# Attention of two transformer blocks: scores issued two steps ahead and between the transposes, loads that hold both heads, reciprocals read with a step of zero

## The reference

```python
def attend(q, k, v, mask, sink):            # first block, both branches
    s = einsum('bqkgd,bskd->bkgqs', q, k) * HEAD_DIM ** -0.5
    if mask is not None: s = where(mask, s, NEG_INF)
    if sink is not None:                    # second branch: one more logit per head
        p = softmax(concat([s, sink]))[..., :-1]
    else:
        p = softmax(s)
    return einsum('bkgqs,bskd->bqkgd', p, v)
# first branch: 8 heads of 64, each query against 512 + 256 keys
# second branch: a window of +-128 keys in blocks of 128, plus the 256 context keys
# layer 0 also attends with the 256 context queries against the 256 context keys
# second block: banded_attention over three dilations (4 heads of 64), combined by their
#   log-denominators, which is one softmax over all their keys; and 8 heads of 96 over 512 keys
```

## Time and profile before

| | |
|---|---|
| median of three executions | 3915.13 us |
| the profiled execution: its time, its span | 3911.86 us, 3910.1 us |
| PE / PEld busy | 3537.8 us (90%) / 2360.5 us (60%) |
| DVE / ACT / POOL busy | 31% / 26% / 5% |
| mean granted TensorE clock | 0.957 |
| scores L1035, PE | 800 matmuls on fp32 data, 167.7 us in the costliest group |
| transposes L1089, PE | 832 + 128 matmuls |
| product L1133, PE | 896 + 128 matmuls |
| reciprocals L1077, DVE | 96, 97.9 us |

### The profile page before, as it was taken

How to read it: one execution, slowest core, us unless ns; L and a number is a source line. 1 busy time by engine, 2 the same in 40 slices (tenths; PEclk the granted TensorE clock), 3 DMA queues, 4 the chain that set the end, 5 groups by cost and what they waited for, 6 DMA issues and landing times.

```text
span 3910.1 us, 48121 instructions
## 1 busy us (share of the span) xinstructions
PE 3537.8 (90%) x21378; PEld 2360.5 (60%) x21378; DVE 1216.6 (31%) x1667; ACT 1020.7 (26%) x1601; POOL 200.2 (5%) x124
## 2 busy tenths in 40 slices
PE   7998889999799999989889988888879888989998
PEld 5786557667663443467658875222237764867886
DVE  3235641112410111134563342111133334344333
ACT  3524531112310000036453231000021335333222
POOL 0100000111200000001000110000001010020000
PEclk9999999999799999989999988999989989999999
DMA  6440004432159999822102324999962010323331
GB/s 211 129 130 12 1 13 132 131 113 70 54 213 383 353 355 386 334 51 81 28 1 77 96 103 166 409 409 409 409 245 70 16 48 17 92 70 88 96 97 49
DMA packets 359982, 600.84 MB, mean 154 GB/s; under 512 B 48770, under 2 KB 242656, under 8 KB 359520
## 3 DMA queue, kind: packets, MB, share of 16 engines
q1 hardware_dynamic: 357024, 596.69, 43.2%
q10 hardware_dynamic: 2752, 1.08, 0.1%
HBM read 595.62 MB, written 2.10 MB: 153 GB/s over the span
## 4 chain that ended last, share of the span: by engine, by line
PE 73%; DVE 10%; DMA 7%; ACT 6%; SPq 3%; issue 1%; POOL 0%; ACTq 0%; POOLq 0%; DVEq 0%
PE ps L554 30%; PE ps L1771 6%; PE ps L2112 4%; DMA ring<-in_w_e_up 3%; PE ps L1280 3%; PE ps L603 3%; DMA ring<-in_w_e_down 3%; SPq L2414 3%; PE ps L1774 3%; PE ps L1803 3%; ACT tmp L1062 3%; DVE sm L1044 3%; PE ps L574 2%; DVE tmp L1077 2%; PE ps L1035 2%; PE ps L1468 2%
## 5 line engine op out<-in xcount | busy, mean ns | idle before, releaser
L554 PE MATMUL ps<-xh,wh 128*128 128x512 f32 x1912 | 647.3, 377 | 39.0 <-DVE xl L1972 16.9
L554 PE MATMUL ps<-xl,wh 128*128 128x512 f32 x1912 | 633.4, 369 | 0.0
L554 PE MATMUL ps<-xh,wl 128*128 128x512 f32 x1912 | 632.2, 369 | 0.0
L529 DVE TENSOR_TENSOR wl<-ring,wh 128x1024 fp32r<-128x1024 f32 (+1 forms) x247 | 309.6, 1254 | 476.6 <-ACT wh L520 476.4
L554 PEld LDWEIGHTS ps<-xh,wh 128*128 128x128 f32 x1912 | 330.8, 190 | 129.8 <-issue 51.6
L520 ACT ACTIVATE wh<-ring 128x1024 fp32r<-128x1024 f32 (+1 forms) x247 | 258.9, 1049 | 431.2 <-PE ps L554 170.1
L554 PEld LDWEIGHTS ps<-xh,wl 128*128 128x128 f32 x1912 | 332.0, 190 | 62.6
L554 PEld LDWEIGHTS ps<-xl,wh 128*128 128x128 f32 x1912 | 330.6, 190 | 62.4 <-issue 4.3
L1771 PE MATMUL ps<-ring,arena 128*32 128x512 f32 x2048 | 269.3, 598 | 1.0 <-DVE arena L1570 1.0
L1766 PE MATMUL ps<-ring,arena 128*64 128x512 f32 x1024 | 236.1, 601 | 29.6 <-DMA ring<-in_w_e_up 14.9
L1089 PE MATMUL ps<-consts,tmp 128*128 128x128 f32 x832 | 127.2, 286 | 70.7 <-DVE arena L1146 55.6
(11 more groups left out here) (246 smaller groups left out, 4492.1 us busy)
## 6 DMA issues: line engine op xcount, KB each, us to landing
ring<-in_w_e_gate SPq DMA_DIRECT2D x128, 1024.0 KB, 9.9
ring<-in_w_e_up SPq DMA_DIRECT2D x128, 1024.0 KB, 10.0
ring<-in_w_e_down SPq DMA_DIRECT2D x128, 1024.0 KB, 11.9
ring<-in_w_in SPq DMA_DIRECT2D x116, 512.0 KB, 4.0
ring<-in_w_ada SPq DMA_DIRECT2D x96, 512.0 KB, 6.1
ring<-in_w_ff SPq DMA_DIRECT2D x64, 512.0 KB, 4.1
ring<-in_w_out SPq DMA_DIRECT2D x24, 512.0 KB, 4.1
ring<-in_w_in SPq DMA_DIRECT2D x40, 256.0 KB, 3.8
```

The source lines that it names most:

```text
L529: e.tensor_tensor(m.WL[:, o:o + many], halves.aps[s][:, 0:many], m.WH[:, o:o + many].bitcast(F32), ALU.subtract).then_inc(*lo.up(X.key, q))
L554: i = e.matmul(ps[0:M, a:b], w[:, k, 0:M], h[:, k, a:b], start=k == 0 and p == 0, stop=k == 7 and p == 2)
```

## The change

It reorders the three loops. PE begins with the scores of steps 0 and 1. In turn i it then issues the transposes of step i, the scores of step i+2, and, if a group ends at i, its product. In such a turn the last load of step i comes after the scores of i+2. ACT copies load 0 of step i and does the exponentials of step i+1. DVE copies all loads from 1 on, then does the reciprocals of step i+1 and the maximum of step i+2, then the product's multiply.

`six` is replaced by `both_heads`: load n holds blocks 2n and 2n+1 of both heads, where before load 0 held four blocks of one head. The product names for each of its terms the load up to which it must wait. The second branch keeps its loads.

The reciprocals are computed once per unit, into the column where the step's maximum stood (`small(i, 0)`), and `RC` is gone. PE reads such a column 64 times (`shares`, a broadcast, step zero) as the weights of four matmuls of 64 output rows in place of two of 128. `dve_soft` waits, before it writes that column again, for the product of the group of step i-4. The copy of the turned reciprocals to SBUF is made by ACT (`act_product`), and DVE multiplies.

```diff
@@ -1015,11 +1015,10 @@
                 s = self.steps[i][0]
                 return sm[:, 16 * (i % 4) + 4 * x:16 * (i % 4) + 4 * x + s["U"]]
 
-            def sums(self, i):
-                s, g = self.steps[i]
-                first = self.ends[g - 1] + 1 if g else 0
-                o = 128 * (i - first)
-                return self.RC[:, 256 * (g % 2) + o:256 * (g % 2) + o + 64 * s["U"]]
+            def shares(self, i, b):
+
+                t = self.small(i, 0).rearrange("p (g b) -> p b g", g=2)[:, b]
+                return [t[:, g:g + 1].broadcast_to([128, 64]) for g in (0, 1)]
 
             def last_load(self, i):
                 return len(self.steps[i][0]["loads"]) - 1
@@ -1040,6 +1039,8 @@
         def dve_soft(e, A, i):
             s = A.steps[i][0]
             mx, ng = A.small(i, 0), A.small(i, 1)
+            if i > 3:
+                e.wait_ge(*a_pv.at(A.stage, A.steps[i - 4][1]))
             e.wait_ge(*a_sc.at(A.stage, i))
...
@@ -1071,52 +1072,42 @@
             if s["sink"] is not None:
                 e.tensor_tensor(A.small(i, 2), A.small(i, 2), A.small(i, 3), ALU.add).then_inc(*a_su.up(A.stage, i))
                 e.wait_ge(*a_su.at(A.stage, i))
-            if g > 1:
-                e.wait_ge(*a_pv.at(A.stage, g - 2))
-            b = s["U"] // 2
-            e.reciprocal(A.sums(i).rearrange("p (b g r) -> p g b r", b=b, g=2),
-                         A.small(i, 2).rearrange("p (g b) -> p g b", g=2).unsqueeze(3).broadcast_to([128, 2, b, 64])).then_inc(*a_rc.up(A.stage, i))
...
+            e.reciprocal(A.small(i, 0), A.small(i, 2)).then_inc(*a_rc.up(A.stage, i))
+
+        def pe_turn(e, A, i, n):
             src = A.units(i, A.P[i % 3])
...
+            ps, when = turned.take((A.stage, i, n), turned_out(A, i, n))
+            for w in when:
+                e.wait_ge(*w)
+            for c, (u, b) in enumerate(A.steps[i][0]["loads"][n][0]):
+                e.wait_ge(*a_ex.at(A.stage, i, u))
+                x = e.transpose(ps[:, 128 * c:128 * c + 128], src[:, u, 128 * b:128 * b + 128], ident)
+            x.then_inc(*a_tr.up(A.stage, i, n))
+
+        def load_sides(A, i, n):
             blocks, dst, shape = A.steps[i][0]["loads"][n]
             ps = turned.of[A.stage, i, n][:, 0:128 * len(blocks)]
...
+            return dst, (ps.rearrange("p (c q) -> p c q", q=128) if shape is None else ps.rearrange("p (g c q) -> p g c q", g=shape, q=128))
 
         def act_turn(e, A, i):
             g = A.steps[i][1]
             if g > 1:
                 e.wait_ge(*a_pv.at(A.stage, g - 2))
...
+            dst, src = load_sides(A, i, 0)
+            e.wait_ge(*a_tr.at(A.stage, i, 0))
+            e.activation(dst, src, ACT.Copy).then_inc(*a_pt.up(A.stage, i))
 
         def dve_turn(e, A, i):
             g = A.steps[i][1]
...
             if g > 1:
                 e.wait_ge(*a_pv.at(A.stage, g - 2))
...
+            for n in range(1, A.last_load(i) + 1):
+                dst, src = load_sides(A, i, n)
+                e.wait_ge(*a_tr.at(A.stage, i, n))
+                e.tensor_copy(dst, src).then_inc(*a_tl.up(A.stage, i, n))
 
         def turned_out(A, i, n):
...
+            return a_tl.at(A.stage, i, n) if n else a_pt.at(A.stage, i)
 
         def pe_product(e, A, g):
             pv = A.groups[g]["pv"]
@@ -1124,26 +1115,31 @@
             ps, when = turned.take((A.stage, "o", g), a_ov.at(A.stage, g))
             for w in when:
                 e.wait_ge(*w)
...
+            for x, (load, heads) in enumerate(pv):
+                for i in range(first, A.ends[g] + 1):
+                    for n in range(min(load, A.last_load(i)) + 1):
+                        e.wait_ge(*turned_out(A, i, n))
                 for r0, v, pt, q0, q1 in heads:
                     e.matmul(ps[r0:r0 + 64, q0:q1], v, pt, start=x == 0, stop=x == len(pv) - 1, skip_group_check=True)
             for b in (0, 1):
...
+                i = first + b if A.ends[g] > first else first
+                e.wait_ge(*a_rc.at(A.stage, i))
+                for h, share in enumerate(A.shares(i, 0 if A.ends[g] > first else b)):
+                    x = e.matmul(ps[64 * h:64 * h + 64, 256 + 128 * b:384 + 128 * b], share, ident,
+                                 start=False, stop=True, skip_group_check=True)
             x.then_inc(*a_pv.up(A.stage, g))
 
+        def act_product(e, A, g):
+            e.wait_ge(*a_pv.at(A.stage, g))
+            if g:
+                e.wait_ge(*a_ov.at(A.stage, g - 1))
+            e.activation(rb, turned.of[A.stage, "o", g][:, 256:512], ACT.Copy).then_inc(*a_rb.up(A.stage, g))
+
         def dve_product(e, A, g):
...
             dst, many = A.groups[g]["out"]
             f = lambda t: t if many is None else t.rearrange("p (b q) -> p b q", b=many)
...
+            e.wait_ge(*a_rb.at(A.stage, g))
+            e.tensor_tensor(dst, f(turned.of[A.stage, "o", g][:, 0:256]), f(rb), ALU.mult).then_inc(*a_ov.up(A.stage, g))
 
         def pe_attention(e, A):
             n = len(A.steps)
@@ -1151,43 +1147,54 @@
                 for w in freed:
                     e.wait_ge(*w)
             turned.start(((), ()))
...
+            pe_scores(e, A, 0)
+            pe_scores(e, A, 1)
+            for i in range(n):
+                last = A.last_load(i)
+                early = last if i in A.ends else last + 1
+                for x in range(early):
+                    pe_turn(e, A, i, x)
+                if i + 2 < n:
+                    pe_scores(e, A, i + 2)
+                for x in range(early, last + 1):
+                    pe_turn(e, A, i, x)
+                if i in A.ends:
+                    pe_product(e, A, A.ends.index(i))
             read = tuple(a_ex.at(A.stage, i, A.steps[i][0]["U"] - 1) for i in (n - 2, n - 1))
             out_ = (a_ov.at(A.stage, len(A.groups) - 1),) + tuple(turned_out(A, n - 1, x) for x in range(A.last_load(n - 1) + 1))
             bank.start((read, read, read, out_))
 
         def act_attention(e, A):
             n = len(A.steps)
...
+            act_soft(e, A, 0)
+            for i in range(n):
+                if i - 1 in A.ends:
+                    act_product(e, A, A.ends.index(i - 1))
+                act_turn(e, A, i)
+                if i + 1 < n:
+                    act_soft(e, A, i + 1)
+            act_product(e, A, len(A.groups) - 1)
 
         def dve_attention(e, A):
             n = len(A.steps)
...
+            dve_soft(e, A, 0)
+            dve_soft(e, A, 1)
+            dve_sums(e, A, 0)
+            for i in range(n):
+                dve_turn(e, A, i)
+                if i + 1 < n:
+                    dve_sums(e, A, i + 1)
+                if i + 2 < n:
+                    dve_soft(e, A, i + 2)
+                if i in A.ends:
+                    dve_product(e, A, A.ends.index(i))
 
         HALF = [slice(0, 64), slice(64, 128)]
 
...
+        def both_heads(PT, qs, many):
+
+            PT = PT.rearrange("p (g c) q -> p g c q", g=2)
+            return [([(g, b) for g in (0, 1) for b in (2 * n, 2 * n + 1)], PT[:, :, 2 * n:2 * n + 2, qs], 2) for n in range(many // 2)]
...
```

More of the change, by code:

```diff
@@ L1001, in build, with __init__ @@
         class Att:
-            def __init__(self, stage, groups, P, PT, RC):
-                self.stage, self.groups, self.P, self.PT, self.RC = stage, groups, P, PT, RC
+            def __init__(self, stage, groups, P, PT):
+                self.stage, self.groups, self.P, self.PT = stage, groups, P, PT
                 self.steps = [(s, g) for g, gr in enumerate(groups) for s in gr["steps"]]
@@ L1126, in pe_product @@
                 e.wait_ge(*w)
-            for i in range(first, A.ends[g] + 1):
-                for n in range(A.last_load(i) + 1):
-                    e.wait_ge(*turned_out(A, i, n))
-                e.wait_ge(*a_rc.at(A.stage, i))
-            for x, heads in enumerate(pv):
+            for x, (load, heads) in enumerate(pv):
+                for i in range(first, A.ends[g] + 1):
+                    for n in range(min(load, A.last_load(i)) + 1):
+                        e.wait_ge(*turned_out(A, i, n))
                 for r0, v, pt, q0, q1 in heads:
@@ L1153, in pe_attention @@
             turned.start(((), ()))
-            for i in range(n + 2):
-                if i < n:
-                    pe_scores(e, A, i)
-                if i > 1 and i - 2 in A.ends:
-                    pe_product(e, A, A.ends.index(i - 2))
-                if 0 < i <= n:
-                    pe_turn(e, A, i - 1)
+            pe_scores(e, A, 0)
[11 more added lines that the diff above has]
+                    pe_product(e, A, A.ends.index(i))
             read = tuple(a_ex.at(A.stage, i, A.steps[i][0]["U"] - 1) for i in (n - 2, n - 1))
@@ L2009, in dilated_attention @@
                     groups.append(dict(steps=steps, pv=pv, out=(to, 2)))
-            return Att("ad", groups, [tmp[:, i * 1536:(i + 1) * 1536] for i in range(3)], PTD, tmp[:, 4608:5120])
```

(1 more changed line is left out.)

75 lines of the change are left out of this document (14 added, 61 removed).

## The result

The changed kernel takes 3821.25 us (median of four executions, 3817.91 to 3825.94); the kernel before took 3910.49 us in the same comparison (four executions, the three of the first section and one of 3902.24). The ratio is 0.9774 [0.9749, 0.9799]: 89 us or 2.3% faster.

A forecast was written before the change was run, and what follows sets the result against it. PE was taken to pace the four attention stages, stopping for DVE. Layer 0 -42, layer 1 -19, latent -9, dilated -1 and small things -3 gave 3911.9 - 74 = 3838 us, range 3808 to 3880.

The forecast's parts named there:

- The cause of the waits: Four attention stages: PE waits through its order and DVE's queue ahead of the multiply; about 2.2 us per layer 1 group.
- The period: First-branch group of layer 1: 9.18 + 0.16 + 0.84 = 10.2 us against 11.40, gaining 1.2 us per group.
- The wait for the multiply: Second load's transposes, layer 1 group: PE waits 0.84 us every time for the multiply to free the product's bank.
- The window pair: Second branch: two window groups take 19.9 us instead of 21.44, with 3.0 us of waits and switches left.
- The latent period: Latent stage: 9.48 - 1.67 + 0.84 + 0.16 + 0.18 = 9.0 us per group.
- The dilated stage: Dilated attention: PE is packed, so nothing gained per group and about 1 us at the ends.
- The clock: Attention stages: denser work keeps PE's granted clock at 0.98 or more; layer 0's shortfall is 15 us of full-rate time.
- A: Rival, 48 groups outside dilated: DVE becomes the bound, a load's copy late behind a reduction; 34 us lost, 3872; chance 0.14.
- B: Rival, 48 groups: clock never falls and the wait for the multiply halves; 20 us more gain, 3818; chance 0.10.
- C: Rival, reciprocal matmuls: eight short passes don't hide weight loads; 22 us, 3860, or 45 us, 3883; chance 0.10.
- D: Rival, reciprocal matmuls: step-zero weight loads as slow as strided ones, fully exposed; 112 us, 3950; chance 0.03.
- E: Rival, whole change: PE's waits only change their names; time stays within 12 us of 3912; chance 0.03.

The follow-up runs named there:

- e4: Changed kernel keeping only the new order: wide reciprocals, one-head loads, reciprocals' copy on DVE and load 1's copy on ACT restored; 3921.40 us, ratio 1.0046.
- e3: Changed kernel with the copy of the turned reciprocals given back to DVE; 3828.42 us, ratio 0.9796.
- e2: Changed kernel with the earlier loads restored, which hold one head in the latent stage; 3831.94 us, ratio 0.9807.
- e5: Kernel before with the short reciprocals alone, in the old order and with the old copies; 3842.23 us, ratio 0.9832.
- e1: Changed kernel with the wide reciprocals restored, written 64 times by DVE and turned by two 128-row matmuls; 3837.12 us, ratio 0.9821.
- e6: Changed kernel with four more short matmuls (eight passes) ahead of the product, weights read at step zero, output unchanged; 3840.19 us, ratio 0.9824.
- e7: Changed kernel with four more short matmuls (eight passes) ahead of the product, weights from 64 plain columns, output unchanged; 3840.31 us, ratio 0.9826.
- e8: Changed kernel with scores cut in halves around the transposes, whole between loads in the latent stage; three-load group ends unchanged; 3803.20 us, ratio 0.9735.

## Why the prediction was right, and where it was not

**The total** was forecast at 3838 us and came out at 3821, inside its range, with 17 us more gain than the likeliest case. The stages were forecast at 202, 164, 60 and 74 us and measured 197, 159, 56 and 68. The total could be right with the cause of the old waits half wrong, since it was added up from PE's pieces in the kernel after; that DVE keeps up there is what this needed, and its margin was counted with the short reciprocals and with load 1 on DVE.

**The cause of the waits: the mechanism was half seen.** The prediction said PE's order and DVE's queue ahead of the multiply made PE wait. PE is indeed what paces the kernel after, and the sum of its pieces was the right way to the period after. But as a cause of the 11.40 us before it was wrong: e4 has the new order and keeps 11.40. The step that failed is the one that wrote off the exchange on DVE: "DVE is not relieved in total; what it wins is the product's copy, which goes to ACT, and the order". Busy time was the wrong measure. The reciprocals gave 66 us alone, and the copy of load 1, booked as a burden of 0.69 us on DVE, gave 51 us alone, since ACT's exponentials no longer queue behind it; of the two things named as winnings, the product's copy is worth 3 us by the stages and 7 by the medians (e3), and the order alone gave nothing (e4).

**The period, 10.2 forecast, 9.80 measured.** Two terms were mis-sized. The wait for the multiply is 0.58, not 0.84: the drain of the reciprocals was taken as 0.31 from T0's start, while ACT's copy begins 0.11 after it (1850.82 and 1850.93). The copy itself (0.38) and the multiply (0.43) were as forecast. And PE has no gap between product and reciprocals: 2.64 us (1857.44 to 1860.08) against 2.74. Together 0.36 of the 0.4.

**Parts that were right.** The reciprocal of two columns takes 0.17 us as estimated (mean 166 ns). The eight short passes take 0.54 (1860.08 to 1860.62), what the four long ones took the earlier trace rows. The groups whose last step has two loads wait for its copy with an idle time of 0.87, and window groups alike, some 1.1 with the quarter that a drain hides, where about 1.0 was forecast; timeline of PE after, a context group of layer 0 and a window group:

```profile
365.45 1.08 PE L1123 MATMUL ps<-arena 128*64 128x256 f32 x8 [0.87 <-DVE arena L1107]
```

```profile
1955.45 2.17 PE L1123 MATMUL ps<-arena 128*64 128x256 f32 x20 [0.88 <-DVE arena L1107]
```

**The window pair** was forecast at 19.9 and is 19.0 (1945.47 to 1964.48): the two terms above, twice (0.7), cover most of it. **The latent period** was forecast at 9.0 and is 8.23:

```profile
3189.75 1.95 PE L1123 MATMUL ps<-tmp,arena 128*64 128x256 f32 x16
...
3195.29 0.60 PE L1084 MATMUL ps<-consts,arena 128*128 128x128 f32 x4
3195.72 1.88 PE L1034 MATMUL ps<-arena 96*128 96x512 f32 x4
3197.44 0.60 PE L1084 MATMUL ps<-consts,arena 128*128 128x128 f32 x4
3197.98 1.95 PE L1123 MATMUL ps<-tmp,arena 128*64 128x256 f32 x16
```

The wait for the multiply and the missing gap behind the product are the two terms above (0.36). The forecast also added 0.18 for the product's second load and 0.16 for a switch: the product begins with no wait, since its first half needs only load 0 (in e2, where it needs both, this stage is 6.9 us longer), and the two loads of four transposes take 0.43 and 0.54 from start to start, less than the 1.02 of the eight in before, so no switch shows. **The dilated stage** was costed at 1 us and gave 3.6. e2 shows 3.4 of them: the loads of both heads spare its products a wait, to which the prediction gave no value there.

**The clock** was 0.94, 0.97, 0.95 and 0.96 and is 0.99, 0.99, 0.97 and 1.00, as forecast (0.98 or more) but for the dilated stage. In layer 0, 0.06 of 244 us was 14.6 us of full-rate time, and 0.01 of 198 is 2. So some 12 of its 46.5 us are clock, by this estimate. It came together with the denser work, which no run separates: the latent stage, where PE was busy for 68.5 of 83 us and is busy for 64.6 of 69, went from 0.96 to 1.00.

**The rivals.** A, a DVE bound: the product waits for no copy in two-step first-branch groups. The reduction does run longer (mean 1748 ns against 1698), which the margin took, but not because ACT reads PSUM beside it: it takes 1738 in e5, which is before with short reciprocals, and 1706 in e1, which is after with wide ones, so it goes with the short reciprocal ahead of it. B: partly true, the wait is 0.58 where 0.84 was forecast and 0.42 was B's. C: out by e6 and e7, and by the 0.54 us of the eight passes in after. The rule that the Trainium skill states (TensorE: Matmul & The Clock Gate, Part 3, The mechanism), that a weight load overlaps running matmuls only when the row group differs, is not borne out by these passes: all use all 128 rows, and eight of them with loads of 135 ns each add 0.44 us. The section's other case, a load into the background weight buffer, would fit; no run tells which it was. D: out by e6 and e7. What the Trainium skill says of cachelines (SBUF — State Buffer, Door 1: The DMA port swizzle) agrees with this as far as it goes: further accesses inside one line run at full rate, and the loads with a step of zero took 135 ns against 136. E: out by the periods.

## What to carry to other kernels

When two engines hand work back and forth, follow one item from engine to engine until it returns to where it began: the sum of these links is the period, however low the busy shares are, and reordering a third engine did not shorten it here. In an engine's in-order list, ask of each instruction that waits what stands behind it: a 0.6 us copy moved to the busier engine gained 51 us here because it no longer held back the exponentials. And where a loop is open already, a second opening is worth less: the reciprocals 66 us alone and 16 on top, load 1 on DVE 51 alone and 35 on top. So parts should be tried alone as well as taken away.

## What the runs showed of the hardware

**Matmuls on the two halves of the rows run side by side, and only as well as their widths match.** The scores of the layers alternate between heads that lie in rows 0 to 63 and 64 to 127. A whole step (256, 512, 512 and 256 columns by turns, 1536 in all) took 1.49 us in before and after, less than the 1024 columns of a latent step, whose two heads take 96 rows each, more than the 128 there are: 1.72 (3195.72 to 3197.44). Split so that 256 columns of one head stand beside 512 of the other, the halves took 1.06 and 1.05 (e8), as if the wider of each pair set the time: less 0.16 for the switch, 1.33 us for 768 columns a head and 0.9 for 512 are both some 1.75 ns a column. That pairing is the reading that fits; no run changed the widths alone.

**A weight load with a step of zero** costs what a plain one does, 135 and 136 ns for 64 columns, while the strided one took 322 ns for 128. **A reciprocal** of two columns takes 166 ns on DVE, and the one of 128 columns 953: where values are repeated, it is cheaper to let the reader repeat them.
